# FFN up products with the high and low input side by side: one 512-column and one 256-column matmul in place of three of 256

## The reference, cut to what matters

```
h = rms_norm(x, ffn_pre_norm[l])
u = h @ w_up                                   # 1024 x 5632
u = sum(up[:, t:t + S] * conv_w[t] for t in range(3))   # depthwise, over tokens
gate, val = split(u, 2)
x = x + rms_norm((gelu(gate) * val) @ w_down, ffn_post_norm[l])
```

## Time and profile before

| what | us |
|---|---|
| median of 3 runs | 1029.37 (1029.29 to 1029.55) |
| span of the profiled execution | 1027.2 |
| TensorE busy in it | 1013.0 |
| VectorE busy | 680.7 |
| ScalarE busy | 587.5 |

### The profile page before, as it was taken

The page is one execution under the profiler, slowest core; times in us unless marked ns, Lnnn a source line. Parts: engine busy times, 40 slices in busy tenths (PEclk is TensorE's granted clock), DMA queues, the critical chain, the costliest instruction groups (busy, mean ns, idle before and its releaser), DMA issues.

```text
span 1027.2 us, 15935 instructions
## 1 busy us (share of the span) xinstructions
PE 1013.0 (99%) x6244; PEld 908.5 (88%) x6244; DVE 680.7 (66%) x932; ACT 587.5 (57%) x859; POOL 130.7 (13%) x257
## 2 busy tenths in 40 slices
PE   8999999999999999999999999999999999999997
PEld 7889999888888999999888899998888889999996
DVE  5635566655596887878865355666555869787877
ACT  5657666565446654555575666565653457455553
POOL 3353124000002000000025221230000020000000
PEclk9999999999999999999999999999999999999999
DMA  8554345444444646555454534464344645545551
GB/s 259 178 177 155 122 141 168 161 165 164 144 150 157 203 169 203 170 200 172 168 190 159 174 124 128 150 205 164 124 144 164 204 145 166 203 169 201 174 195 41
DMA packets 109037, 170.78 MB, mean 166 GB/s; under 512 B 3377, under 2 KB 72804, under 8 KB 108964
## 3 DMA queue, kind: packets, MB, share of 16 engines
q1 hardware_dynamic: 107676, 166.88, 48.8%
q10 hardware_dynamic: 1208, 2.63, 0.7%
q0 software_dynamic: 80, 0.26, 0.1%
HBM read 168.72 MB, written 1.05 MB: 165 GB/s over the span
## 4 chain that ended last, share of the span: by engine, by line
PE 95%; DVE 1%; ACT 1%; DMA 1%; issue 1%; DVEq 0%; SPq 0%; POOL 0%; POOLq 0%
PE bank L1418 28%; PE bank L1420 28%; PE bank L1419 28%; PE bank L1783 2%; PE bank L1684 1%; PE bank L1705 1%; PE bank L1776 1%; PE bank L1693 1%; PE bank L1721 1%; PE bank L1728 1%; PE bank L1773 1%; DMA w_raw<-in_w_in_dram 1%; PE bank L1735 1%; PE bank L1741 1%; DVE x_rows L1233 0%
## 5 line engine op out<-in xcount | busy, mean ns | idle before, releaser
L1053 DVE TENSOR_TENSOR w_lo<-w_raw,w_hi 128x2048 fp32r<-128x2048 f32 (+3 forms) x174 | 364.3, 2094 | 160.6 <-ACT w_hi L700 160.5
L700 ACT ACTIVATE w_hi<-w_raw 128x2048 fp32r<-128x2048 f32 (+3 forms) x174 | 304.7, 1752 | 50.3 <-PE bank L1420 48.8
L1418 PE MATMUL bank<-w_hi,hT_lo 128*128 128x512 f32 (+2 forms) x700 | 258.4, 369 | 1.5 <-DVE hT_lo L1127 0.8
L1420 PE MATMUL bank<-w_hi,hT_hi 128*128 128x512 f32 (+2 forms) x700 | 252.9, 361 | 0.0
L1419 PE MATMUL bank<-w_lo,hT_hi 128*128 128x512 f32 (+2 forms) x700 | 252.5, 361 | 0.0
L1418 PE MATMUL bank<-hT_hi,w_lo 128*128 128x256 f32 x704 | 199.4, 283 | 0.7 <-DVE hT_lo L1080 0.7
L1420 PE MATMUL bank<-hT_hi,w_hi 128*128 128x256 f32 x704 | 199.2, 283 | 0.0
L1419 PE MATMUL bank<-hT_lo,w_hi 128*128 128x256 f32 x704 | 199.2, 283 | 0.0
L1418 PEld LDWEIGHTS bank<-w_hi,hT_lo 128*128 128x128 f32 x700 | 131.5, 188 | 17.8 <-issue 3.0
L1420 PEld LDWEIGHTS bank<-w_hi,hT_hi 128*128 128x128 f32 x700 | 131.4, 188 | 14.1
L1419 PEld LDWEIGHTS bank<-w_lo,hT_hi 128*128 128x128 f32 x700 | 131.6, 188 | 13.0
(11 more groups left out here) (215 smaller groups left out, 1250.1 us busy)
## 6 DMA issues: line engine op xcount, KB each, us to landing
w_raw<-in_w_up_dram SPq DMA_DIRECT2D x44, 1024.0 KB, 4.9
w_raw<-in_w_in_dram SPq DMA_DIRECT2D x36, 1024.0 KB, 4.9
w_raw<-in_w_in_dram SPq DMA_DIRECT2D x36, 768.0 KB, 4.2
w_raw<-in_w_down_dram SPq DMA_DIRECT2D x22, 1024.0 KB, 4.8
w_raw<-in_w_out_dram SPq DMA_DIRECT2D x8, 1024.0 KB, 4.9
w_raw<-in_w_in_dram SPq DMA_DIRECT2D x8, 672.0 KB, 4.0
w_raw<-in_w_branch_mla_dram SPq DMA_DIRECT2D x4, 1024.0 KB, 4.9
w_raw<-in_w_branch_diff_dram SPq DMA_DIRECT2D x4, 1024.0 KB, 4.8
```

What stands on the lines that cost most here:

```text
L700: nc.scalar.activation(w_hi[:, n % RING, 0:nk * cols], raw[:, n % RING, 0:nk * cols], ACT.Copy).then_inc(hi_done, 1)
L1053: V.tensor_tensor(w_lo[:, n % RING, s], raw[:, n % RING, s], w_hi[:, n % RING, s].bitcast(F32), ALU.subtract).then_inc(lo_done, 1)
L1418: PE.matmul(dst, lhs[1], rhs_hi, start=start, stop=False)
L1420: return PE.matmul(dst, lhs[0], rhs_hi, start=False, stop=stop)
```

## The change

`hT_hi` and `hT_lo` become the two halves of one tensor `hT`, so that for one input block both can be read as 512 moving columns. For every up piece but c = 0, `passes` is replaced by `passes_beside`: for each (tile, block) one matmul of the high weights against [high | low] input (512 columns into a whole bank) and one of the low weights against the high input (256 columns into the bank's left half). The right half of the bank then holds high weights x low input, and the two halves must be added. A piece takes two banks (4, 5 for even c; 6, 7 for odd c). ScalarE waits for the piece and copies both right halves to `up_low`, VectorE waits for that copy and adds it to the left halves into `up_scaled`, drains, and multiplies by the scales in place. TensorE waits with piece c until the sum of piece c - 2 is made (c = 2: until piece 0 is scaled).

```diff
-        hT_hi = sb("hT_hi", [P, KD, SEQ], F32R)
-        hT_lo = sb("hT_lo", [P, KD, SEQ], F32R)
+        hT = sb("hT", [P, 2, KD, SEQ], F32R)
+        hT_hi, hT_lo = hT[:, 0], hT[:, 1]
...
+            up_low = sb("up_low", [P, 2, SEQ], scope=four)
...
-            return bank[4 + c % 4][:, j * SEQ:(j + 1) * SEQ]
+        def up_banks(c):
+
+            return high_banks[:, 2 * (c % 2):2 * (c % 2) + 2, :]
...
                         if kind == "up":
                             u, b = c // 2, c % 2
+                            if c:
+                                act.wait_ge(piece_used, l * NPIECE + (RING + n + 1))
+                                nc.scalar.activation(up_low[:], up_banks(c)[:, :, SEQ:2 * SEQ], ACT.Copy).then_inc(up_low_copied, 1)
                             act.wait_ge(up_scaled_done, l * 2 * NU + (c + 1))
...
-                    last = V.tensor_tensor(up_scaled[:, c % 2, :, :], bank[4 + c % 4][:].rearrange("p (j q) -> p j q", j=2),
+                    dve.wait_ge(up_low_copied, l * (2 * NU - 1) + c)
+                    V.tensor_tensor(up_scaled[:, c % 2, :, :], up_banks(c)[:, :, 0:SEQ], up_low[:], ALU.add).then_inc(up_summed, 1)
+                    dve.drain()
+                    last = V.tensor_tensor(up_scaled[:, c % 2, :, :], up_scaled[:, c % 2, :, :],
                                            token_scale.rearrange("p (o q) -> p o q", o=1).broadcast_to([P, 2, SEQ]), ALU.mult)
...
+            def passes_beside(dst, w_parts, k):
+
+                if k == 0:
+                    PE.matmul(dst, w_parts[0], hT[:, :, k, :], start=True, stop=False)
+                last = PE.matmul(dst[:, 0:SEQ], w_parts[1], hT_hi[:, k, :], start=False, stop=False)
+                if k:
+                    last = PE.matmul(dst, w_parts[0], hT[:, :, k, :], start=False, stop=k == KD - 1)
+                return last
...
-                    if c >= 4:
-
-                        pe.wait_ge(up_scaled_done, l * 2 * NU + (c - 3))
+                    if c == 2:
+
+                        pe.wait_ge(up_scaled_done, l * 2 * NU + 1)
+                    if c >= 3:
+
+                        pe.wait_ge(up_summed, l * (2 * NU - 1) + (c - 2))
```

More of the change, by code:

```diff
@@ L373, in build_trunk @@
             par_rows = sb("par_rows", [44, 4 * DEPTH, P], scope=six)
-        bank = [ctx.enter_context(nc.psum_tensor(f"bank{i}", [P, 512], F32)) for i in range(8)]
+        bank = [ctx.enter_context(nc.psum_tensor(f"bank{i}", [P, 512], F32)) for i in range(4)]
+        high_banks = ctx.enter_context(nc.psum_tensor("high_banks", [P, 4, 512], F32))
+        bank += [high_banks[:, i, :] for i in range(4)]
         S_BANK, O_BANK = (bank[4], bank[5]), bank[7]
@@ L415, in build_trunk @@
         root_rows_ready, scales_full, up_scaled_done = sem("root_rows_ready"), sem("scales_full"), sem("up_scaled_done")
+        up_low_copied, up_summed = sem("up_low_copied"), sem("up_summed")
         lat_squares, lat_normed = sem("lat_squares"), sem("lat_normed")
@@ L498, in turned_bank, with first_half @@
             return bank[((0, 1, 6, 7), (2, 3, 5, 0))[t][k // 2]][:, (k % 2) * P:(k % 2 + 1) * P]
-        def up_half(c, j):
-            if c == 0:
-                return bank[(4, 2)[j]][:, 0:SEQ]
-            return bank[4 + c % 4][:, j * SEQ:(j + 1) * SEQ]
+        def first_half(j):
+            return bank[(4, 2)[j]][:, 0:SEQ]
+        def up_banks(c):
+            return high_banks[:, 2 * (c % 2):2 * (c % 2) + 2, :]
         root_rows = xn[:, 0, 0:NT * P].rearrange("p (t q) -> p t q", t=NT)
@@ L1098, in scale_up @@
             def scale_up(l, n, c):
-                dve.wait_ge(piece_used, l * NPIECE + (RING + n + 1))
                 if c == 0:
+                    dve.wait_ge(piece_used, l * NPIECE + (RING + n + 1))
                     scale_rows(l)
                     for j in range(2):
-                        last = V.tensor_tensor(up_scaled[:, c % 2, j, :], up_half(c, j), token_scale, ALU.mult)
+                        last = V.tensor_tensor(up_scaled[:, c % 2, j, :], first_half(j), token_scale, ALU.mult)
                 else:
-                    last = V.tensor_tensor(up_scaled[:, c % 2, :, :], bank[4 + c % 4][:].rearrange("p (j q) -> p j q", j=2),
+                    dve.wait_ge(up_low_copied, l * (2 * NU - 1) + c)
+                    V.tensor_tensor(up_scaled[:, c % 2, :, :], up_banks(c)[:, :, 0:SEQ], up_low[:], ALU.add).then_inc(up_summed, 1)
+                    dve.drain()
+                    last = V.tensor_tensor(up_scaled[:, c % 2, :, :], up_scaled[:, c % 2, :, :],
                                            token_scale.rearrange("p (o q) -> p o q", o=1).broadcast_to([P, 2, SEQ]), ALU.mult)
@@ L1505, in use_piece @@
                             turn_roots(l)
-                        last = passes(up_half(c, j), (hi[:, k, j * P:(j + 1) * P], lo[:, k, j * P:(j + 1) * P]),
-                                      hT_hi[:, k, :], hT_lo[:, k, :], k == 0, k == 7)
+                        w_parts = (hi[:, k, j * P:(j + 1) * P], lo[:, k, j * P:(j + 1) * P])
+                        if c == 0:
+                            last = passes(first_half(j), w_parts, hT_hi[:, k, :], hT_lo[:, k, :], k == 0, k == 7)
+                        else:
+                            last = passes_beside(up_banks(c)[:, j, :], w_parts, k)
                     last.then_inc(piece_used, 1)
```

## The result

| | us |
|---|---|
| before, median of 4 runs | 1029.46 (1029.29 to 1029.57) |
| changed kernel, median of 4 runs | 1044.91 (1044.62 to 1045.18) |
| ratio | 1.015, 95% interval 1.0138 to 1.0162 |
| spans of the profiled executions | 1027.2 and 1043.3 |

The change makes the kernel 15.4 us slower. The forecast was 14.5 slower, 1043.9.

The account below looks back on a forecast made before the run. TensorE bounds the kernel before; VectorE's lengthened work would turn the loop after the change. Per layer 2.7 + 2.6 + 1.95 = 7.25 us, twice +14.5, on 1029.4 gives 1043.9 us, range 1036 to 1051.

Parts of the forecast that it names:

- the 1.66 and 1.78 us by which VectorE was ahead: Steady period: VectorE's margins before TensorE wants the low part of g and the next E's split weights.
- the list: VectorE's work from E's end to the next E's split weights; forecast 2.21 us longer.
- E0 to E3: First units, no down piece between early up pieces to give VectorE time: 2.7 us later per layer.
- E3 to E10: Seven steady periods per layer, each 17.36 us against 16.98: 2.6 us more.
- E10 to end of D10: Last units: the last down pieces wait for VectorE's low parts of g, 1.95 us more per layer.
- the walk: Step-by-step timing of VectorE's work after E ends at S, giving a new period of 17.36 us against 16.98.
- the matmuls: Up pieces: 0.0133 us less per tile and block, a piece 5.55 instead of 5.76 us.
- VectorE's loop: E ends, VectorE's work, next E's low part ready, TensorE runs it; claimed to set the period, 17.36 us.
- (a): Rival: VectorE keeps ahead in the steady units and the kernel gets faster, 1020.4 us; 6%.
- (b): Rival: gain and loss nearly cancel if the product from SBUF runs at half of 0.68 us, 1030 us; 4%.
- (c): Rival: the wider matmuls save nothing, through the two-part operand or the width switch, 1047.2 us; 15%.
- (d): Rival: TensorE's stalls at E and D lower its clock, adding over 150 us; 2%.

Follow-up runs that it names:

- e3: Changed kernel with only the order altered: from unit 2 on VectorE makes D's low part ahead of the sum of E; 1032.77 us, ratio 1.0034.
- e4: Changed kernel without ScalarE's copy: VectorE waits for the piece itself and adds the scales' rows instead, result incomplete; 1031.13 us, ratio 1.0019.
- e1: Changed kernel with the wider matmuls alone, no copy or sum, result incomplete; 1022.67 us, ratio 0.9935 against the kernel before.
- e2: Changed kernel with copy and sum kept but three 256-column matmuls again, result complete; 1048.26 us, ratio 1.0184 against the kernel before.
- e6: Matmuls-alone kernel with high and low input of a block contiguous, result incomplete; 1022.71 us, ratio 0.9934 against the kernel before.
- e7: Matmuls-alone kernel with the two tiles of a piece swapped from c = 2 on, result incomplete; 1022.38 us, ratio 0.9933 against the kernel before.

## Why the prediction was right

**The bound.** The step on which all else rests was that the 1.66 and 1.78 us by which VectorE was ahead, and not its 34% of idle time, are what the change may spend. The change grew the list by 2.17 us (S+9.45 to S+11.62 at the end of the split of the next E; 2.21 forecast). e3 and e4 show it from both sides: taking 2.2 us of other work out of that list brings the period back to TensorE's own 16.63, and taking out 0.6 us of waiting brings it to 16.75. The profile's page alone would have said that an engine with a third of its time free can take a 0.69 us sum in 8 us.

**The terms**, counted from the first matmul of E0 (layer 1: 328.07 before, 328.65 after; layer 2: 832.87 and 841.40):

| term | forecast | layer 1 | from | layer 2 | from |
|---|---|---|---|---|---|
| E0 to E3 | +2.7 | +3.06 | 40.54 before; 372.25 - 328.65 = 43.60 | +2.72 | 40.53 before; 884.65 - 841.40 = 43.25 |
| E3 to E10 | +2.6 | +2.79 | 118.86 before; 493.90 - 372.25 = 121.65 | +2.75 | 118.86 before; 1006.26 - 884.65 = 121.61 |
| E10 to end of D10 | +1.95 | +2.10 | 28.16 before; 524.16 - 493.90 = 30.26 | +2.09 | to the last matmul: 27.77 before; 1036.12 - 1006.26 = 29.86 |
| layer | +7.25 | +7.95 | | +7.56 | |

The starts of E3 and E10, and of the first transpose after D10, in the changed kernel, layer 1, then of E3 and E10 in layer 2:

```profile
372.25 0.50 PE L1437 MATMUL high_banks<-hT,w_hi 128*128 128x512 f32 x1 [0.72 <-DVE w_lo L1062]
...
493.90 0.50 PE L1437 MATMUL high_banks<-hT,w_hi 128*128 128x512 f32 x1 [0.30 <-DVE w_lo L1062]
...
524.16 1.23 PE L1592 MATMUL high_banks<-ident,x_rows 128*128 128x128 f32 x8
...
884.65 0.50 PE L1437 MATMUL high_banks<-hT,w_hi 128*128 128x512 f32 x1 [0.37 <-DVE w_lo L1062]
...
1006.26 0.50 PE L1437 MATMUL high_banks<-hT,w_hi 128*128 128x512 f32 x1 [0.32 <-DVE w_lo L1062]
```

The two layers differ at E3 by 0.34 us. In layer 1 VectorE stands still between the taps of E2, for nothing that the profile shows, and in layer 2 it does not:

```profile
365.82 0.88 DVE L1381 SCALAR_TENSOR_TENSOR conv_out<-up_scaled,par_all,conv_out 128x255 f32<-128x255 f32 x2
367.13 0.88 DVE L1387 SCALAR_TENSOR_TENSOR conv_out<-up_scaled,par_all,conv_out 128x255 f32<-128x255 f32 x2 [0.43 <-issue]
...
878.57 0.88 DVE L1381 SCALAR_TENSOR_TENSOR conv_out<-up_scaled,par_all,conv_out 128x255 f32<-128x255 f32 x2
879.52 0.88 DVE L1387 SCALAR_TENSOR_TENSOR conv_out<-up_scaled,par_all,conv_out 128x255 f32<-128x255 f32 x2
```

From one tap to the next it is 1.31 us there and 0.95 in layer 2; the walk had no such pause. So layer 2 hit the term of 2.7 and layer 1 did not. Both layers together are +15.5 us.

**The one term mis-sized** is the matmuls: 5.55 us for a piece, measured 5.59 (e1), so that 42 pieces save 7.1 and not 9.0 us. It was bounded by 5.76. In VectorE's loop it adds 0.04 us to each period and somewhat to the ends; the same walk with 5.59 gives +15.1 us in place of +14.5, and +15.4 was measured. In the Trainium skill, "TensorE: Matmul & The Clock Gate" gives the figure by which 1.7 us could be saved in all (section "Back-to-back issue gap") for a single matmul, and says itself that it comes out too low at small widths where each matmul has a weight load. This kernel has such a stream, and e1 saves 6.7 us: the figure was the wrong one to hold against the rows.

**Rivals.** (a) fell: the list grew by more than 1.4 us. (b) fell: the product from SBUF took 0.69 us. (c), no gain per matmul, was shown wrong by e1, which has 0.17 of the 0.21 us per piece. (d) fell: the granted clock is full in every slice, with a wait in every period.

**What it got wrong in small.** I expected gaps of 0.6 to 0.9 us before each E. The trace calls it 0.30 to 0.32, because it counts from a matmul's modelled end; by starts it is 0.69 (406.32, the last of D2, to 407.01) where 0.227 is usual, so 0.46 late. The rest of the 0.8 had been lost at D and in restarting. D itself starts 0.30 us after the matmul before it (400.69 to 400.99), 0.07 late, too little to stand in the trace as a wait. The copy starts 0.20 us after a piece's end, not 0.25; it is the 0.04 to 0.06 us by which the whole list runs ahead of the walk.

The head of the kernel, which the change doesn't touch, gave another 0.57 us in this one profile (its first product at 11.56 instead of 10.99 us); in the profiles of e1 to e4 it lies between 11.20 and 11.51. The cause is open. It explains the spans: 15.5 us of the two layers and 0.57 of the head are the 16.1 by which they differ, where the forecast had 14.5.

## What to carry to other kernels

Work added to an engine costs nothing only while it fits into the time by which that engine is ahead at each thing that others wait for. Find that time by walking one period from the event that starts the engine's list to the moment its result is wanted; idle time elsewhere in the period doesn't count, until work is moved into it. And where such a list is full, its order is worth as much as its length: one low part moved from behind a wait to ahead of it returned 12 us without an instruction less.

## What the runs showed of the hardware that was not expected

In a stream of 512 and 256 column matmuls, eight pairs to a tile, slow and fast tiles take turns: 2.81 to 2.82 us for one, 0.352 a pair, and 2.77 to 2.78 for the next, 0.347 a pair, in every layout and order tried (e1, e6, e7). Only across D0 do two slow ones follow each other.
